# Routing a mixture of experts from raw token rows, with the next layer's row sums on GpSimd

## The reference

```python
h = rms_norm(x, norm_ffn[l])                       # x * rsqrt(mean(x*x) + 1e-6) * gain
lg = h @ w_rg + b_rg                               # 4 group logits
grp = argmax(lg); p_grp = softmax(lg)[grp]
le = (h @ w_re + b_re).reshape(n_tok, 4, 8)[grp]   # 8 expert logits of that group
top_p, top_i = lax.top_k(softmax(le), 2)
gate = top_p / sum(top_p) * p_grp
y = sum over the two experts of gate * ((silu(h @ w_eg[e]) * (h @ w_eu[e])) @ w_ed[e])
x = x + y
...
mod = einsum('bd,sde->sbe', silu(c), ada_w[i]) + ada_b[i][:, None, :]   # second block
shift, scale, gate = split(mod, 3)                 # for each of two sites
h = x * (1 + scale) + shift
```

## Time and profile before

| | |
|---|---|
| median of 3 runs | 2379.17 us |
| lowest and highest run | 2373.69, 2382.54 us |
| profiled execution, first to last instruction | 2380.9 us |
| TensorE busy | 2265.6 us (95%) |
| VectorE busy | 1813.5 us (76%) |
| ScalarE busy | 1150.8 us (48%) |
| GpSimd busy | 132.0 us (6%) |
| DMA | 572.51 MB, mean 240 GB/s |

### The profile page before, as it was taken

One profiled execution on the slowest core, in us unless ns is written; L12 is line 12 of the kernel. 1 busy time (PEld: TensorE's weight loads), 2 busy tenths in 40 slices (PEclk: granted clock), 3 DMA queues, 4 the chain that ended last, 5 costly groups with the idle time before them and its releaser, 6 DMA issues. The chain is left out here.

```text
span 2380.9 us, 30361 instructions
## 1 busy us (share of the span) xinstructions
PE 2265.6 (95%) x11981; PEld 1913.7 (80%) x11981; DVE 1813.5 (76%) x2133; ACT 1150.8 (48%) x1197; POOL 132.0 (6%) x229
## 2 busy tenths in 40 slices
PE   7999888999999999989999989999998999898997
PEld 7888677878888888878788887888987888797886
DVE  6887686478888888866788777887796888777545
ACT  4443244367767676744443254432653434364332
POOL 2000100000000000000111000110001111000000
PEclk9999988899999999999999999999999999999999
DMA  8844552489999999964699634996543898344662
GB/s 299 283 124 131 174 176 89 114 300 373 370 356 371 356 369 363 364 211 156 180 376 366 220 125 134 371 371 221 174 136 124 283 376 313 121 143 154 191 193 71
DMA packets 347057, 572.51 MB, mean 240 GB/s; under 512 B 68128, under 2 KB 181280, under 8 KB 346912
## 3 DMA queue, kind: packets, MB, share of 16 engines
q1 hardware_dynamic: 326176, 495.02, 61.5%
q0 software_dynamic: 20736, 75.51, 8.4%
HBM read 569.39 MB, written 1.05 MB: 240 GB/s over the span
## 5 line engine op out<-in xcount | busy, mean ns | idle before, releaser
L286 DVE TENSOR_TENSOR st_lo<-st_raw,st_hi 128x2048 fp32r<-128x2048 f32 (+1 forms) x195 | 441.0, 2267 | 117.5 <-ACT st_hi L276 117.2
L286 DVE TENSOR_TENSOR es_lo<-es_raw,es_hi 128x2048 fp32r<-128x2048 f32 x192 | 429.3, 2286 | 75.9 <-ACT es_hi L276 74.6
L276 ACT CAST st_hi<-st_raw 128x2048 fp32r<-128x2048 f32 (+1 forms) x195 | 368.4, 1892 | 232.5 <-PE ps L316 157.4
L314 PE MATMUL ps<-st_hi,sb_h_hi 128*128 128x512 f32 (+1 forms) x1232 | 462.9, 376 | 15.7 <-DVE sb_h_lo L1139 7.9
L316 PE MATMUL ps<-st_hi,sb_h_lo 128*128 128x512 f32 (+1 forms) x1232 | 453.1, 368 | 0.0
L315 PE MATMUL ps<-st_lo,sb_h_hi 128*128 128x512 f32 (+1 forms) x1232 | 452.9, 368 | 0.0
L276 ACT CAST es_hi<-es_raw 128x2048 fp32r<-128x2048 f32 x192 | 357.6, 1910 | 52.5 <-DMA es_raw<-in_w_expert_up_dram 25.5
L314 PEld LDWEIGHTS ps<-st_hi,sb_h_hi 128*128 128x128 f32 x1232 | 234.1, 190 | 58.4 <-issue 13.0
L316 PEld LDWEIGHTS ps<-st_hi,sb_h_lo 128*128 128x128 f32 x1232 | 233.9, 190 | 38.7
L315 PEld LDWEIGHTS ps<-st_lo,sb_h_hi 128*128 128x128 f32 x1232 | 234.4, 190 | 35.4
L314 PE MATMUL ps<-es_hi,moe_hg_hi 128*128 128x512 f32 x512 | 205.7, 402 | 5.1 <-PEq L61 5.1
(11 more groups left out here) (690 smaller groups left out, 3769.0 us busy)
## 6 DMA issues: line engine op xcount, KB each, us to landing
st_raw<-in_ffn_w_in_dram SPq DMA_DIRECT2D x176, 512.0 KB, 6.7
t_aw<-in_ada_w_dram POOLq DMA_DIRECT2D x144, 512.0 KB, 7.0
es_raw<-in_w_expert_gate_dram SPq DMA_DIRECT2D x64, 1024.0 KB, 8.2
es_raw<-in_w_expert_up_dram SPq DMA_DIRECT2D x64, 1024.0 KB, 7.4
es_raw<-in_w_expert_down_dram SPq DMA_DIRECT2D x64, 1024.0 KB, 7.3
st_raw<-in_ffn_w_out_dram SPq DMA_DIRECT2D x44, 1024.0 KB, 9.1
fb_aw<-in_ada_w_dram SPq DMA_DIRECT2D x39, 512.0 KB, 5.8
hs_raw<-in_w_in_dram SPq DMA_DIRECT2D x36, 512.0 KB, 7.3
```

Source lines behind the costliest of these rows:

```text
L276: act.copy(p.at(self.hi[:, m % self.held, :]), p.at(self.raw[:, n % self.slots, :])).then_inc(self.high, 1)
L286: dve.tensor_tensor(p.at(self.lo[:, m % self.held, :]), p.at(self.raw[:, n % self.slots, :]), p.at(self.hi[:, m % self.held, :]).bitcast(F ...
L314: pe.matmul(out, a_hi, b_hi, start=start, stop=False, skip_group_check=True)
```

## The change

Routing starts from X itself. TensorE transposes raw rows, the gain of the norm (now a column of 128x8, `M.gain`) multiplies the router's weights, and the root multiplies the logits. The gathered columns get the gain as ScalarE and VectorE copy them; high and low rows are gathered into one bank and split again. The ranks are computed right behind the group's choice. GpSimd splits the first three weight pieces in place of VectorE, and SyncE sends eight pieces in this stage in place of five. The column and row sums for the second block leave TensorE: GpSimd makes them with sums over partitions (`site_rows`) in the experts' stage, where SyncE, after 48 pieces, waits for these sums to be read and loads two bias rows.

```diff
         @block.sync
         def _(sp):
             with nc.allow_non_contiguous_dma("small vectors"):
-                sp.dma_start(gain[:], rows(A["norm_ffn"][0])).then_inc(q["gained"], 16)
+                sp.dma_start(M.gain[:], column(A["norm_ffn"][0])).then_inc(q["gained"], 16)
                 for dst, src in smalls:
                     sp.dma_start(dst, src).then_inc(q["small"], 16)
             S.send(sp, lent)
-            mod.load(sp)
+            sp.wait_ge(q["squared"], NT)
+            S.send(sp, lent + 1)
             sp.wait_ge(q["logits"], 1)
-            for c in range(2):
-                mine_row.load(sp, c)
-            next_row.load(sp, 0)
-            sp.wait_ge(q["low"], NT)
-            S.send(sp, S.slots)
-            next_row.load(sp, 1)
+            S.send(sp, S.slots + 3)
+            with nc.allow_non_contiguous_dma("small vectors"):
+                for dst, src in site_loads(k, A):
+                    sp.dma_start(dst, src).then_inc(M.site_landed, 16)
...
             for t in range(NT):
                 pool.wait_ge(q["spread"], t + 1)
                 pool.tensor_tensor(ss[:, t:t + 1], ss[:, t:t + 1], k.nhalf[:, 0:1], ALU.pow).then_inc(q["rooted"], 1)
+            S.lower(pool, 3)
...
         def _(pe):
-            mod.sums(pe, 1)
-            for t in range(NT):
-                pe.wait_ge(q["normed"], t + 1)
+            for t in range(NT):
                 for i in range(8):
-                    last = pe.transpose(ps[:, 2 * t + i // 4, i % 4 * P:(i % 4 + 1) * P], h[:, t, i * P:(i + 1) * P],
+                    last = pe.transpose(ps[:, 2 * t + i // 4, i % 4 * P:(i % 4 + 1) * P], X[:, t, i * P:(i + 1) * P],
...
+            stir(k, pe, 5, 4)
+            pe.wait_ge(q["scaled"], 1)
             for t in range(NT):
...
-                    last = pe.matmul(ps[:, 4, t * 36:(t + 1) * 36], hT[:, i, t * P:(t + 1) * P], wr[:, i, :],
-                                     start=i == 0, stop=i == 7)
+                    last = pe.matmul(logit(t), hT[:, i, t * P:(t + 1) * P], wr[:, i, :], start=i == 0, stop=i == 7)
             last.then_inc(q["logits"], 1)
-            for c in range(2):
-                mine_row.sum(pe, c)
-            next_row.sum(pe, 0)
-            stir(k, pe, 0, 8)
+            stir(k, pe, 5, 6)
...
-            for n, (w, i) in enumerate(jobs):
-                if n >= 4:
-                    pe.wait_ge(q["g_hi" if w == 0 else "g_lo"], n // 2 - 1)
+            for i in range(8):
+                if i >= 4:
+                    pe.wait_ge(q["g_lo"], i - 3)
+                for w in range(2):
+                    for t in range(NT):
+                        last = pe.matmul(ps[:, i % 4, :], (h_hi, h_lo)[w][:, t, i * P:(i + 1) * P],
+                                         perm[:, t, 0:NG, :].rearrange("p j s -> p (j s)"), start=w == t == 0,
+                                         stop=w == 1 and t == NT - 1)
+                last.then_inc(q["gathered"], 1)
+            for j in range(NJ):
                 for t in range(NT):
-                    last = pe.matmul(ps[:, n % 4, :], (h_hi, h_lo)[w][:, t, i * P:(i + 1) * P],
-                                     perm[:, t, 0:NG, :].rearrange("p j s -> p (j s)"), start=t == 0, stop=t == NT - 1)
-                last.then_inc(q["gathered"], 1)
+                    last = pe.transpose(ps[:, 4 + j // 2, j % 2 * T + t * P:j % 2 * T + (t + 1) * P],
+                                        perm[:, t, j, :].bitcast(F32), k.ident[:])
+            last.then_inc(q["turned_perm"], 1)
...
             for t in range(NT):
-                act.wait_ge(q["normed"], t + 1)
-                act.copy(h_hi[:, t, :], h[:, t, :]).then_inc(q["high"], 1)
                 act.wait_ge(q["turned"], 2 * t + 1)
                 act.copy(hT[:, 0:4, t * P:(t + 1) * P], ps[:, 2 * t, :].rearrange("p (k s) -> p k s", k=4)
                          ).then_inc(q["copied0"], 1)
+            for t in range(NT):
+                act.wait_ge(q["rooted"], t + 1)
+                act.activation(h_hi[:, t, :], X[:, t, :], ACT.Copy, scale=ss[:, t:t + 1]).then_inc(q["high"], 1)
+            S.lift(act, 3)
...
+            act.wait_ge(q["gained"], 16)
+            for i in range(8):
+                act.wait_ge(q["gathered"], i + 1)
+                act.activation(M.hg_hi[:, 0:NG, i, :], ps[:, i % 4, :].rearrange("p (j s) -> p j s", j=NG), ACT.Copy,
+                               scale=M.gain[:, i:i + 1]).then_inc(q["g_hi"], 1)
...
-            dve.wait_ge(q["gained"], 16)
-            for t in range(NT):
-                dve.wait_ge(q["rooted"], t + 1)
-                dve.scalar_tensor_tensor(h[:, t, :], X[:, t, :], ss[:, t:t + 1], gain[:], ALU.mult, ALU.mult
-                                         ).then_inc(q["normed"], 1)
-            for t in range(NT):
                 dve.wait_ge(q["turned"], 2 * t + 2)
                 dve.tensor_copy(hT[:, 4:8, t * P:(t + 1) * P], ps[:, 2 * t + 1, :].rearrange("p (k s) -> p k s", k=4)
                                 ).then_inc(q["copied1"], 1)
+            dve.wait_ge(q["gained"], 16)
+            dve.wait_ge(q["small"], 16 * len(smalls))
+            dve.tensor_tensor(wr[:], wr[:], M.gain[:].unsqueeze(2).to_broadcast([P, 8, 36]), ALU.mult
+                              ).then_inc(q["scaled"], 1)
             for t in range(NT):
                 dve.wait_ge(q["high"], t + 1)
-                dve.tensor_tensor(h_lo[:, t, :], h[:, t, :], h_hi[:, t, :].bitcast(F32), ALU.subtract
-                                  ).then_inc(q["low"], 1)
+                dve.scalar_tensor_tensor(h_lo[:, t, :], X[:, t, :], ss[:, t:t + 1], h_hi[:, t, :].bitcast(F32), ALU.mult,
+                                         ALU.subtract).then_inc(q["low"], 1)
...
             dve.wait_ge(q["logits"], 1)
-            after(dve.tensor_tensor(lt[:], ps[:, 4, 0:NT * 36].rearrange("p (t n) -> p t n", t=NT),
-                                    br[:].unsqueeze(1).to_broadcast([P, NT, 36]), ALU.add))
+            for t in range(NT):
+                op = dve.scalar_tensor_tensor(lt[:, t, :], logit(t), ss[:, t:t + 1], br[:], ALU.mult, ALU.add)
+            after(op)
             lg, le = lt[:, :, 0:NG], lt[:, :, NG:36].rearrange("p t (g e) -> p t g e", g=NG)
             after(dve.tensor_reduce(mg[:], lg, AX.X, ALU.max))
             first(lg, mg[:], pick[:], NG).then_inc(q["picked"], 1)
             dve.wait_ge(q["picked"], 1)
             after(dve.tensor_tensor(wide[:], le, pick[:].unsqueeze(3).to_broadcast([P, NT, NG, NE]), ALU.mult))
             after(dve.tensor_reduce(mine[:], wide[:].rearrange("p t g e -> p t e g"), AX.X, ALU.add))
+            dve.wait_ge(q["ranked"], 1)
+            after(dve.tensor_tensor(cum[:], ranks[:, 0:NT, :], pick[:], ALU.mult))
+            after(dve.tensor_reduce(b1[:], cum[:], AX.X, ALU.add))
+            dve.tensor_scalar(rk[:, :, 0:NG], cum[:], -1.0, None, ALU.add)
+            after(dve.tensor_scalar(rk[:, :, NG:].rearrange("p t o -> p (t o)"), b1[:], -1.0 - P, None, ALU.add))
+            dve.tensor_tensor(perm[:].rearrange("p t j s -> p (t j) s"), slots[:].unsqueeze(1).to_broadcast([P, NT * NJ, P]),
+                              rk[:].rearrange("p t j -> p (t j)").unsqueeze(2).to_broadcast([P, NT * NJ, P]),
+                              ALU.is_equal).then_inc(q["placed"], 1)
             after(dve.tensor_reduce(m1[:], mine[:], AX.X, ALU.max))
             after(first(mine[:], m1[:], one[:], NE))
...
+            def lower(i):
+                dve.wait_ge(q["g_hi"], i + 1)
+                dve.scalar_tensor_tensor(M.hg_lo[:, 0:NG, i, :], ps[:, i % 4, :].rearrange("p (j s) -> p j s", j=NG),
+                                         M.gain[:, i:i + 1], M.hg_hi[:, 0:NG, i, :].bitcast(F32), ALU.mult,
+                                         ALU.subtract).then_inc(q["g_lo"], 1)
+            dve.tensor_scalar(count[:], ranks[:, NT, :], float(P), None, ALU.is_gt)
+            lower(0)
             after(first(mine[:], m2[:], two[:], NE))
-            dve.wait_ge(q["ranked"], 1)
-            after(dve.tensor_tensor(cum[:], ps[:, 4, 0:NT * NG].rearrange("p (t g) -> p t g", t=NT), pick[:], ALU.mult))
-            after(dve.tensor_reduce(b1[:], cum[:], AX.X, ALU.add))
-            dve.tensor_scalar(rk[:, :, 0:NG], cum[:], -1.0, None, ALU.add)
-            after(dve.tensor_scalar(rk[:, :, NG:].rearrange("p t o -> p (t o)"), b1[:], -1.0 - P, None, ALU.add))
-            dve.tensor_tensor(perm[:].rearrange("p t j s -> p (t j) s"), slots[:].unsqueeze(1).to_broadcast([P, NT * NJ, P]),
-                              rk[:].rearrange("p t j -> p (t j)").unsqueeze(2).to_broadcast([P, NT * NJ, P]),
-                              ALU.is_equal).then_inc(q["placed"], 1)
...
+def bias_loads(k, A, thirds):
+    return [(row, rows(A["ada_b_2"][0, site][2048:3072])) for site, row in ((1, thirds[2]), (0, k.gates[:, 0, :]))]
+def site_rows(k, pool, thirds, sums, cols, reduced, landed, step):
+    c, site = k.cols, 1
```

(87 more changed lines are left out.)

81 lines of the change are left out of this document (29 added, 52 removed).

## The result

The changed kernel takes 2394.1 us (median of 4 runs, 2391.0 to 2396.5), the kernel before 2380.9 beside it: ratio 1.0058, 95% interval 1.0035 to 1.0081. It is slower by 0.6%. The profiled execution took 2391.0 us, with a span of 2389.2 against 2380.9. The medians lie 13.2 us apart and the two profiles 8.3; what follows explains the profiles.

What follows compares the result with a forecast made beforehand. Routing was bound by one chain of short steps, the experts by TensorE while VectorE's splits keep up. Routing's 4.0 us saved minus 1 lost beside the experts, off the profiled 2380.9 (1.7 above the median), gave 2376; range 2355 to 2425.

Steps and rivals of the forecast that it cites:

- C: Experts' stage: GpSimd's sums hold VectorE as its multiply does; 33 us lost at three plain passes, total 2408; chance 0.26.
- The stage of routing: Routing: GpSimd's three splits, 5.2 us each, block VectorE's chain until about 465; the stage still ends 4.0 us earlier.
- Case A: Routing: GpSimd's splits cause no block that counts; 18.8 us saved, total 2360; chance 0.30.
- The step that failed: Experts' stage: GpSimd's sums let VectorE go on, 20.5 us of other blocking meets 19.5 of spare; +1 us.
- the power's rows: Profile rows beside GpSimd's power: no two-input VectorE instruction over 0.485 us, so a long GpSimd instruction need not hold VectorE.
- The spare: Experts' stage: VectorE can absorb blocking with 8.5 us of lead plus 0.133 of the time it lasts.
- The short instructions: Experts' stage: GpSimd's products, trees, column steps and row passes block VectorE for 20.5 us, costing +1.
- 3.5a + 5: Experts' stage: estimated loss in us if the sums hold VectorE, which is then blocked for 20.5 + 4a us.
- a: Experts' stage: time of one GpSimd sum over partitions of 128x1024, bounded between 1 and 179 us.
- Experts' start: Start of the experts' stage, with three pieces split: counted as nothing, at most 1.4 us of gain from a shorter pause.
- SyncE's stop: Experts' stage: with sums of 21 to 100 us, SyncE's wait before piece 48 holds the stream; about 2480; chance 0.06.
- Case E: Experts' stage: a sum takes 100 us or more, SyncE stands 400 us or longer; 2780 and up; chance 0.03.

Runs made afterwards that it cites:

- e1: Changed kernel with GpSimd's three splits of weight pieces given back to VectorE; 2389.8 us, ratio 1.0034 to the kernel before.
- e8: e1 with SyncE issuing the second site's three column loads ahead of the logits; 2385.3 us, ratio 1.0012 to the kernel before.
- e11: Kernel before with only an unused tile of 64 bytes per partition added ahead of the split weights; 2383.9 us, ratio 1.0014.
- e10: Kernel before with only an unused tile of 32 bytes per partition added ahead of the split weights; 2373.5 us, ratio 0.9985.
- e3: Changed kernel keeping GpSimd's four sums over partitions but without trees, column steps and row passes; 2386.7 us, ratio 1.0033 to the kernel before.
- e5: Changed kernel with the first two of four GpSimd sums done three times, eight in all; 2407.1 us, ratio 1.0105 to the kernel before.
- e2: Changed kernel without GpSimd's sums, trees, column steps and row passes beside the experts; 2372.2 us, ratio 0.9973 to the kernel before.
- e4: Changed kernel without GpSimd's four sums over partitions, keeping trees, column steps and row passes; 2381.4 us, ratio 1.0003 to the kernel before.

## Why the prediction was wrong

I had said 2376, range 2355 to 2425, with 0.36 on slower. Of the cases C happened, in the lower part of its times: the sums hold VectorE.

- **The stage of routing** was right in its mechanism, the block by GpSimd's splits (e1, e8), and near in its number by luck: 4.0 us less forecast, 4.4 measured. Counted from the stage's start, `rt_perm` ended after 29.7 us, forecast 30.6, and two errors met in that. I had taken 5.2 us for a split on GpSimd and it took 4.48, so GpSimd was done after 25.1 us, not 28.5; but from there to the end of `rt_perm` it took 4.6 us, not 2.2, because TensorE's rank matmuls could only start then. The stage before was a draw as well: its code took 50.1 us in e11 and 41.2 in e10, at another granted clock (last section), while the new code took 45.8 to 46.5 in five profiles. Against an execution like e10's the new routing would be 4.6 us longer, not 4.4 shorter. And the 0.65 of the earlier trace rows, which I read as the clock after pauses, is of a stretch in which TensorE was in flight for 19.21 of 19.30 us. The new stage shows the pause: 9.48 us idle, and 0.50. The Trainium skill ("SBUF — State Buffer", "Who interferes with whom") gave this lock, and this trace agrees for the splits (4.42 and 4.22 us on 8 columns), while beside the power, which reads SBUF too, no instruction was held. Case A's 31.4 us without a block was too low: e8 took 35.4.
- **The step that failed** is "If the sums behave so, 20.5 us of blocking meet about 19.5 of spare: +1, my value." I chose by the power's rows that a sum over partitions lets VectorE go on. It does not: a split beside one takes 6.62 us, and the sums cost 13.6 us for four of 6.1 to 6.5 (e3), 14.2 for four more (e5). In place of +1 the work cost 17.9 us (e2). The power's rows were no guide to it. Perhaps because the power reads 16 or 24 columns and a sum 1024; no run tests that.
- **The spare** was sized too high as well. The short instructions alone, forecast at +1, cost 4.7 (e4), though they blocked VectorE only 10.2 us, not 20.5. My reading is that a spare of 13.3% on average does not cover blocks that come in bursts; no run separates that.
- **Case C's formula**, 3.5a + 5, gives 28.9 at the measured mean a of 6.83 us; the work cost 17.9. It took 20.5 + 4a = 47.8 us as block; VectorE's splits lost 24.0. GpSimd waits for VectorE too: six halvings took 15.38 us beside it, while in e4 the first six, with VectorE idle during most of them, took 5.63 and the next six, beside its splits, 11.53. Timeline of POOL in e4:

```profile
486.92 5.63 POOL L1612 TENSOR_TENSOR third<-third 128x512 f32<-128x512 f32 x6
...
495.40 11.53 POOL L1612 TENSOR_TENSOR third<-third 128x512 f32<-128x512 f32 x6
```

- **Experts' start**, "at most 1.4 us of gain": the stage gained 4.9, for another reason, the tiles' place (e10). Without this chance the change would have ended near 2399, an estimate from 2394.1 and 4.9.
- **SyncE's stop** (case D) did not come: the last sum over a gate row ended at 564.2, and SyncE issued the biases at 610.9, behind piece 47. The switches of GpSimd's code showed as gaps of 7.5 to 8.7 us before its next instruction ("issue"), more than the 6 us or so that the Trainium skill gives for the first call of freshly loaded code ("GPSIMD Engine Reference", "Instruction dispatch"), and cost the path nothing that these runs show: four sums cost 3.4 us each in e3 and, with no further switch, 3.5 in e5. Case E fell: a was 6.8, not 100. Its price was off by its own terms, too: at a = 100 SyncE would stand 314 us (11.6 + 23 + 400 - 120.8), not 400.

In the profiles: 4.4 less, 17.9 more, 4.9 less is 8.6 more, of 8.3. By the medians the change costs 13.2 us, and e2 puts the work beside the experts at 21.9. The runs of the kernel before spread over 12 us, more than these differences of 4 to 5; they stay open.
